# Block 1's first norms: eight leading tiles on x times the norm weight, the token factor put on their PSUM banks

## The reference

```
def rmsnorm(x, g):
    y = x * lax.rsqrt(jnp.mean(x * x, axis=-1, keepdims=True) + EPS)
    return y * g

xn = rmsnorm(x, norm1_g[l])
proj = xn @ w_in                      # 1024 x 9472: gdn_qkv (2048 columns), gates and others
gdn_qkv = silu(causal_dwconv(gdn_qkv, conv_w))     # four taps per channel
q, k = l2norm(...), l2norm(...)                    # then the gated delta rule
```

## Time and profile before

| | us |
|---|---|
| median of 3 runs (lowest, highest) | 2471.23 (2468.78, 2472.56) |
| the profiled execution | 2476.37 |
| its span | 2474.5 |
| PE busy | 2375.8 (96%) |
| DVE, ACT, POOL busy | 1432.0, 1246.8, 301.3 |
| first product of the lead, layer 0 | 16.80 |
| first product of the lead, layer 1 | 671.92 |

### The profile page before, as it was taken

How to read it: one execution, slowest core, us unless ns; L and a number is a source line. 1 busy time by engine, 2 the same in 40 slices (tenths; PEclk the granted TensorE clock), 3 DMA queues, 4 the chain that set the end, 5 groups by cost and what they waited for, 6 DMA issues and landing times.

```text
span 2474.5 us, 48016 instructions
## 1 busy us (share of the span) xinstructions
PE 2375.8 (96%) x21242; PEld 2197.9 (89%) x21242; DVE 1432.0 (58%) x2151; ACT 1246.8 (50%) x1846; POOL 301.3 (12%) x171
## 2 busy tenths in 40 slices
PE   6989999999999899899999999999999999998999
PEld 6979898999899798899999787887789998787999
DVE  6773875665467467756655247643335553676554
ACT  5745654554466475456544367542223453445543
POOL 5213000000141220001000004200000001331000
PEclk9999999999999999999999999999999999999999
DMA  5344354555444444445553336333325542223555
GB/s 195 127 155 169 137 179 151 198 184 190 164 170 149 153 160 147 173 142 204 189 186 122 119 107 219 119 119 137 119 85 188 205 155 88 81 93 137 176 190 181
DMA packets 55824, 380.98 MB, mean 154 GB/s; under 512 B 6081, under 2 KB 9665, under 8 KB 10305
## 3 DMA queue, kind: packets, MB, share of 16 engines
q1 hardware_dynamic: 54864, 374.59, 42.2%
q10 hardware_dynamic: 752, 3.33, 0.4%
HBM read 375.79 MB, written 1.05 MB: 152 GB/s over the span
## 4 chain that ended last, share of the span: by engine, by line
PE 75%; DVE 12%; ACT 7%; DMA 3%; issue 2%; POOL 0%; DVEq 0%; ACTq 0%; POOLq 0%
PE ps L950 20%; PE ps L951 19%; PE ps L952 19%; DVE r L2241 4%; ACT r L1577 2%; DMA ring<-in_win 2%; PE ps L1031 1%; PE ps L1032 1%; PE ps L1033 1%; PE ps L1079 1%; PE ps L909 1%; PE ps L871 1%; PE ps L988 1%; DVE slab L2330 1%; PE ps L989 1%
## 5 line engine op out<-in xcount | busy, mean ns | idle before, releaser
L950 PE MATMUL ps<-r,r 128*128 128x256 f32 (+1 forms) x4448 | 1321.0, 297 | 11.9 <-DVE r L2241 3.1
L951 PE MATMUL ps<-r,r 128*128 128x256 f32 (+1 forms) x4448 | 1306.5, 294 | 0.0
L952 PE MATMUL ps<-r,r 128*128 128x256 f32 (+1 forms) x4448 | 1305.9, 294 | 0.0
L2241 DVE TENSOR_TENSOR r<-ring,r 128x1024 fp32r<-128x1024 f32 x554 | 678.6, 1258 | 508.9 <-ACT r L1577 508.5
L950 PEld LDWEIGHTS ps<-r,r 128*128 128x128 f32 x4448 | 838.2, 188 | 49.5 <-issue 13.3
L952 PEld LDWEIGHTS ps<-r,r 128*128 128x128 f32 x4448 | 837.9, 188 | 24.9
L951 PEld LDWEIGHTS ps<-r,r 128*128 128x128 f32 x4448 | 838.3, 188 | 24.4 <-issue 0.5
L1577 ACT ACTIVATE r<-ring 128x1024 fp32r<-128x1024 f32 (+1 forms) x610 | 610.1, 1041 | 276.2 <-DMA ring<-in_fo 61.7
L3176 POOL TENSOR_TENSOR slab<-slab 128x512 f32<-128x512 f32 (+1 forms) x20 | 28.7, 1433 | 1234.4 <-ACT slab L1693 1214.1
L3128 POOL TENSOR_TENSOR r<-ring,r 128x1024 fp32r<-128x1024 f32 x56 | 132.7, 2393 | 226.1 <-ACT r L1577 216.2
L2330 DVE SCALAR_TENSOR_TENSOR slab<-ps,v,slab 128x255 f32<-128x255 f32 (+1 forms) x168 | 67.8, 475 | 76.0 <-ACT slab L1645 76.0
(11 more groups left out here) (348 smaller groups left out, 2522.5 us busy)
## 6 DMA issues: line engine op xcount, KB each, us to landing
ring<-in_win SPq DMA_DIRECT2D x74, 1024.0 KB, 4.8
ring<-in_ada SPq DMA_DIRECT2D x48, 1024.0 KB, 4.8
ring<-in_fi SPq DMA_DIRECT2D x44, 1024.0 KB, 4.8
ring<-in_fo SPq DMA_DIRECT2D x36, 1024.0 KB, 4.7
ring<-in_wup SPq DMA_DIRECT2D x32, 1024.0 KB, 4.7
ring<-in_wdn SPq DMA_DIRECT2D x32, 1024.0 KB, 4.7
ring<-in_hin SPq DMA_DIRECT2D x20, 1024.0 KB, 4.7
ring<-in_nqkv SPq DMA_DIRECT2D x12, 1024.0 KB, 4.8
```

The lines of the kernel that those rows point to most:

```text
L950: self.mm(o, hi[:, k - k0, cs], xh, k == 0, False)
L951: self.mm(o, hi[:, k - k0, cs], xl, False, False)
L952: i = self.mm(o, lo[:, k - k0, cs], xh, False, k == last)
L2241: self.tt(K.low(p), K.raw(p), K.high(p).bitcast(F32), ALU.subtract).then_inc(*self.up("w_lo_v", p))
```

## The change

In both layers the first eight tiles of `qkv` (`raw=8`) are multiplied with `xg`, the split of x * g, in place of `xn`. The token factor is put on afterwards: for each of these four banks DVE multiplies the bank in place by `rs` before ACT writes the last tap. `xn` is still made, for everything from `wsm` and tile 8 on.

- In layer 0 ACT loads x itself, in three pieces, with a small load of the norm weight ahead; SP's first unit is split in two loads; the low parts of chunks 0 and 1 are made by DVE in place of POOL. The constants, vectors and other inputs are loaded one unit later.
- PE runs 20 products of ones, 128 columns each, at the start (`awake`).
- In layer 1 `xg` is made tile pair by tile pair while `wdn` of layer 0 adds to x, on ACT and DVE.
- The order of turns: `norm1` is in three steps, with the lead, the product with ones, and tiles 2 and 3 between; `normed` stands behind the first bank's taps; tiles 4 to 7 come before `wsm`; `ada0` of layer 1 comes behind `wsm`; the transposes stand behind tiles 8 and 9, and both `angles` turns, tiles 10 and 11 and the chain to `dA` between them and `cum`, which follows tile 11 at once as before.

```diff
+    def source(self, K, tile):
+        if tile < self.more.get("raw", 0):
+            return K.xg, lambda k: ("n_v", ("lo", ("g", self.layer), k))
+        return self.x, self.xk
...
-        win("qkv", 0, 16, "conv", lead=2, dst=self.g_acc, taps="gw", bias=None, free=[])
+        win("qkv", 0, 16, "conv", lead=2, raw=8, dst=self.g_acc, taps="gw", bias=None, free=[])
...
-    if L:
-        yield ("ada0", 1)
-    yield from [("norm1", None), ("qkv", 2), ("small", 1), ("qkv", 1), ("small", 2), *first(("angles", 1)), ("qkv", 1), ("small", 1), *first(("angles", 1)),
-                ("qkv", 1), *first(("angles", 1)),
-                ("qkv", 1), ("small", 1), *first(("conditions", None)), ("qk", 1), ("qkv", 1), ahead("z", 1), ...
+    yield from [("norm1", 1), ("qkv", 1), ("norm1", 1), ("qkv", 1), ("norm1", None), ("qkv", 2), ("small", 1), *([("ada0", 1)] if L else []),
+                ("qkv", 1), ("small", 2), *first(("angles", 1)), *first(("angles", 1)), ("qkv", 1), ("small", 1), *first(("angles", 1)), ("small", 1), *first(("conditions", None)), ("qk", 1), ("qkv", 1), ahead("z", 1), ...
...
+    def awake(self):
+        P = self.open("awake")
+        for _ in range(AWAKE):
+            self.mm(P[:, 0:128], self.K.one, self.K.one, True, True)
...
     def start(self):                                   # ScalarE
-        self.wait_ge(self.K.sem("x"), 16)
-        self.wait_ge(*self.at("misc_g", "eps"))
+        K = self.K
+        self.e.dma_start(K.gain, K.d["v1"][:, 0, 0:8]).then_inc(K.sem("gain"), 16)
+        for n, (a, b) in enumerate(XIN):
+            self.e.dma_start(K.x[:, a:b, :], K.d["x"][:, a:b, :]).then_inc(K.sem(f"x{n}"), 16)
+        self.e.preload_act_table_set(LN_EXP)
...
+    def gained(self, L, a, b):                         # ScalarE
+        for j in range(a, b):
+            self.act(K.xg[0][:, j, :], K.x[:, j, :], ACT.Copy, scale=K.gain_of(L)[:, j:j + 1])...
...
     def norm(self, pid, own):                          # ScalarE
         if own:
+            for n, (a, b) in enumerate(XIN):
+                self.wait_ge(K.sem(f"x{n}"), 16)
+                self.gained(0, a, b)
+                if n < 2:
+                    self.first(n)
             self.power_own(pid, K.x, T)
...
+        yield
+        self.root(pid, K.rs[:, 0, :], T, 1 / 1024)
         yield
         self.highs(pid, K.sq, K.xn, 8)
...
     def conv(self, job):                               # VectorE
+                if g < job.more.get("raw", 0):
+                    self.wait_ge(*self.at("dense_p", job.key, g))
+                    self.wait_ge(*self.at("n_s", "rs", ("n1", job.layer)))
+                    self.tt(P, P, bc(self.K.rs[:, 0:1, :], [128, m, T]), ALU.mult)...
...
     def onto_x(self, job, g, m, P):                    # VectorE
+        if job.more["power"] == ("n1", 1):
+            self.wait_ge(*self.mine("ev_v"))
+            self.gained(1, g, g + m)
...
     def gained(self, L, a, b):                         # VectorE
+        for j in range(a, b):
+            self.stt(K.xg[1][:, j, :], K.x[:, j, :], K.gain_of(L)[:, j:j + 1], K.xg[0][:, j, :].bitcast(F32), ALU.mult, ALU.subtract)...
```

More of the change, by code:

```diff
@@ L21 @@
 HI = 4
+AWAKE = 20
 AHEAD = 2
@@ L259, in rings @@
             h = 2 * (split[self.unit_of[p]] % 2) + c % 2
-            self.hi_of[p], self.hi_before[p], self.by_pool[p] = h, at.get(h), mat == "win" and c < 28
+            self.hi_of[p], self.hi_before[p], self.by_pool[p] = h, at.get(h), mat == "win" and c < 28 and p > 1
             at[h] = p
@@ L300, in power_wide, with gain_of @@
         return 512 if pid == ("n1", 2) else T
+    def gain_of(self, L):
+        return self.V1[1]["n1"] if L else self.gain
     def presummed(self, pid):
@@ L409, in block1_memory @@
         self.mixed, self.gate, self.y, self.sq, self.rs = (A(8, T) for _ in range(5))
-        self.one = self.mixed[:, 0, 0:128]
+        self.one = self.gate[:, 0, 0:128]
+        at = SHIFT + 2 * 8 * T
+        self.xg = [blocks(self.rounded(at + i, 8 * T), 8) for i in (0, 2 * 8 * T)]
         self.few = self.gate[:, 1:2, :]
@@ L971, in lead @@
         halves, got = job.more.get("halves"), {}
+        source, have = job.source(K, 0)
         if halves:
@@ L975, in lead @@
             whole, by_tile = slice(0, n), job.more.get("by_tile", kt)
-            order = [(whole, job.xk, t, k) for k in range(by_tile) for t in range(tiles)]
-            order += [(whole, job.xk, t, k) for t in range(tiles) for k in range(by_tile, kt)]
+            order = [(whole, have, t, k) for k in range(by_tile) for t in range(tiles)]
+            order += [(whole, have, t, k) for t in range(tiles) for k in range(by_tile, kt)]
         for cs, xk, t, k in order:
@@ L1755, in norm @@
         if own:
-            self.power_own(pid, K.x, T)
-            self.e.preload_act_table_set(LN_EXP)
-            self.first(0)
-            self.log(pid, K.rs[:, 0, :], T, 1 / 1024)
-            self.roots(pid, K.rs[:, 0, :])
-            self.first(1)
-        else:
-            self.root(pid, K.rs[:, 0, :], T, 1 / 1024)
+            self.wait_ge(K.sem("gain"), 16)
+            for n, (a, b) in enumerate(XIN):
[3 more added lines that the diff above has]
+                    self.first(n)
+            self.power_own(pid, K.x, T)
+        yield
+        if own:
+            self.wait_ge(*self.at("misc_g", "eps"))
+        self.root(pid, K.rs[:, 0, :], T, 1 / 1024)
         yield
@@ L1814, in angles @@
             self.wait_ge(*self.at("misc_v", name))
-            self.act(tab, K.y[:, 2, :] if name == "cos" else K.y[:, 4, :], ACT.Sin).then_inc(*self.up("misc_s", name))
+            self.act(tab, K.around[:, 2, :] if name == "cos" else K.around[:, 4, :], ACT.Sin).then_inc(*self.up("misc_s", name))
             yield
@@ L2430, in norm @@
             self.tt(both[:, 0, :], both[:, 0, :], both[:, 1, :], ALU.add).then_inc(*self.up("n_v", "sum", pid))
-            for p in range(2):
-                self.first(p)
+        yield
         yield
@@ L2455, in angles @@
         self.ts(ang, pos, K.V1[0]["inv"], None, ALU.mult).then_inc(*up("misc_v"))
-        for name, shift, kk, r in (("cos", 0.25, K.y[:, 1, :], K.y[:, 2, :]), ("sin", 0.0, K.y[:, 5, :], K.y[:, 4, :])):
+        for name, shift, kk, r in (("cos", 0.25, K.around[:, 1, :], K.around[:, 2, :]), ("sin", 0.0, K.around[:, 5, :], K.around[:, 4, :])):
             self.wait_ge(*mine("misc_v"))
@@ L3276, in program @@
             at = 2 * (u % RAW) * SLOT
+            if u == 0:
+                e.dma_start(K.ring[:, 0:SLOT], src[:, 0:SLOT]).then_inc(K.sem("head"), 16)
+                e.dma_start(K.ring[:, SLOT:2 * SLOT], src[:, SLOT:2 * SLOT]).then_inc(K.raw_sem(chunks[1]), 16)
+                continue
             e.dma_start(K.ring[:, at:at + src.shape[1]], src).then_inc(K.raw_sem(chunks[0]), 16)
```

47 lines of the change are left out of this document (31 added, 16 removed).

## The result

| | before | forecast | after |
|---|---|---|---|
| median, us | 2471.89 (4 runs) | 2482 (2466 to 2491) | 2498.30 (4 runs, 2496.74 to 2501.76) |
| profiled execution / its span | 2476.37 / 2474.5 | 2487.3 | 2501.76 / 2499.9 |
| pieces of x at ACT, layer 0 | 6.33 (whole) | 4.3, 5.3, 7.4 | 9.80, 12.76, 17.00 |
| product with ones | 10.48 | 16.2 | 24.64 |
| tile 6, layer 0 | | 32.7 | 41.35 |

The ratio after to before is 1.0112, 95% interval 1.0099 to 1.0124. The direction was right, the size was not: the time lies 7 us above the top of the range. The spans differ by 25.4 us: +15.6 up to tile 14 of layer 0, -1.4 from there to the end of `wdn` (590.0 in place of 591.4), +11.7 from there to tile 14 of layer 1, -0.5 behind it.

The account below looks back on a forecast made before the run. PE, busy 96% of the span, was taken as the bound, so only its pauses and low clock count. Layer 0 +3.2 and layer 1 +7.7 gave +10.9 us on 2471.2: 2482, range 2466 to 2491.

Parts of the forecast that it names:

- Start of layer 0: Layer 0's start: x arrives in pieces by 7.4, the lead ends at 15.6 in place of 24.2, a gain of 8.6 us.
- the fifth rival: Start: x not earlier because it shares with the weights, first products 2 us later, 2484; chance 0.56 together with the forecast.
- I take no spell: Between products of ones and lead, layer 0: no low-clock stretch after pauses of 0.9 and 1.7 us; 1.5 to 2.8 otherwise.
- A new wait at tile 6: Tile 6, layer 0 and again layer 1: PE waits 4.7 us (4 to 5.5) for chunk 6, prepared behind `xn`.
- A longer wait at `cum`: `cum` of layer 0: PE waits 10 us (5.5 to 11.7) where it waited 2.27, one bank covering in place of three.
- Step into layer 1: From `wdn` into layer 1: PE goes straight into the lead, 665.0 to 670.6 at full clock; tile 7 ends at 694.5.
- A wait for the ring: Tile 8 of layer 1: the load of chunks 8 and 9 is issued late, PE waits 4.3 us (3.5 to 4.7).
- `cum` of layer 1: At `cum` in layer 1, without angles: PE waits 3.8 us (2 to 5) for the chain to `dA`.
- a spell 1.5: Behind a new pause: products run at 1.2 GHz for a while, priced at 1.5 us from a span of 1.5 to 2.8.
- my fourth rival: Slower still: each of five pauses is followed by 29 products at 1.2 GHz, +6.5 us over the forecast, 2489; chance 0.17.
- Nothing is given back: Behind tile 14: old order, DVE's and ACT's chains as late as PE, so none of the added time is recovered.

Follow-up runs that it names:

- The remedies: Two runs, each against the changed kernel: x loaded from SP's queue, 2491.55 us; SP's second unit held back until x is there, 2494.40 us.
- the fastest kernel: Changed kernel plus x on SP, chunks 6 and 7 ahead, `ada0` behind, `cum` later, and chunks of `wsm`, 8, 9 right behind `xn`: 2469.38 us, ratio 0.9985.

## Why the prediction was right in direction and too small

By the spans 25.4 us were measured and 10.9 forecast: 14.5 are missing.

**Step "Start of layer 0": wrong, 8.4 of the 14.5 us.** I took the pieces of x at 4.3, 5.3 and 7.4, "with -1 to +2 us on all", because all of x landed by 6.33 when it went ahead of everything. It no longer does: the new order asks for x and 4.2 MB of SP's at once. The pieces came 5.5, 7.5 and 9.6 us later than that, and the product with ones at 24.64 in place of 16.2; from it to tile 6 the forecast holds (16.7 against 16.5). That the lateness is sharing is shown by the run in which the second unit waits. The Trainium skill, "DMA: Bandwidth & Descriptors", section on queues, rings and completion order, has each DMA engine taking its issuers' rows in turn, a packet at a time. The traces agree: in the run with x in one load, whose first 25 us hold no other loads, SP's 4.18 MB are 864 packets of the profile and ACT's 1.05 MB 1184; taken in turn x, a fifth of the bytes, must be the last to land, and it was (16.8 there, 17.0 in the changed kernel). I had cited it and put it at 2 us, and the fifth rival named this case at the same price: the mistake was not to divide the bytes asked for by the rate in the earlier trace rows, 295 GB/s, which gives 18 us for 5.2 MB (the first us without a byte included). The remedies give back 4 of the 8.4 us; the rest of the step's miss stays open.

**"I take no spell" behind the products of ones: wrong.** The pauses were 4.9 and 1.9 us and the clock was at 1.2 GHz behind both. The forecast's 1.5 us for a warm start were not there, as the run with one product shows.

**"A new wait at tile 6": right.** 4.81 and 4.83 against 4.7 (4 to 5.5), released by POOL's low part, and the edit that moves chunks 6 and 7 ahead removes it. The forecast priced only the first wait: `wsm` is late behind it, a second pause in the shadow of the first.

**"A longer wait at `cum`": right in place, at the far end in size.** 11.6 against 10 (5.5 to 11.7). I had allowed POOL two or three holds of 2.3 and taken 65; three came, two in the second chain of angles and one on `dA` itself. From the transposes to `cum` 18.8 us passed, 2.0 more than forecast.

**Step into layer 1: right.** PE goes straight from `wdn` into the lead, and no time is lost or won against the forecast up to tile 6 (22.9 against 22.4).

**"A wait for the ring": right.** 4.69 against 4.3 at tile 8, and moving `ada0` takes it away. `cum` of layer 1: 4.5 against 3.8.

**Term "a spell 1.5" (low clock): too small, about 4 of the 14.5 us.** From tile 6 to the transposes 16.7 us passed in layer 0 where five tiles at full clock take 14.0; I had added 1.5. The five stretches behind the pauses, without the pauses, took 1.2, 0.4, 0.2, 0.8 and 1.1 us more than forecast. The forecast took the short end of the earlier trace rows; my fourth rival (the text also calls it the third) took the long end for all, and its 6.5 us were a little nearer to these 3.7. The Trainium skill, "TensorE: Matmul & The Clock Gate", Part 1, says that the number of products at the lower clock varies between runs; the runs agree: 25 products lie 0.21 us apart behind the pause at tile 6 of layer 0, 16 behind that of layer 1 and 21 behind tile 8's. A forecast of five pauses must take the middle, not the end.

**"Nothing is given back" behind tile 14: not contradicted.** The two stretches came out 1.4 and 0.5 us shorter. But such stretches differ by 8 us and more between profiles of kernels with the same order there, so that they are this near is partly luck.

Sum: forecast +10.9; start +8.4, tile 6 and clock +1.4, up to `cum` of layer 0 +2.0 and behind it +0.4, layer 1 +4.0, the rest -1.9: 25.2 of the 25.4 measured. The range had given the start only 2 us above, and one step shifted everything behind it. The forecast had +3.2 for layer 0 and +7.7 for layer 1 and measured were +15.6 and +11.7: right in sign and in where PE waits, wrong in the size of the start above all.

## What to carry to other kernels

When a load is moved to another queue, add up all the bytes asked for at the same time, by every queue, and divide by the rate the trace shows; a load's old landing time belongs to its old place in the order. Count the cover at both ends of what is moved: the new order starts the lead early and leaves one bank of cover in place of three at `cum`, and single turns of the list (two chunks prepared earlier, `ada0` later) won 7.8 and 4.8 us by the marks. A removed pause is judged by what is late next, so measure from mark to mark in the profile, not by totals alone, and set the last mark behind the stage that the edit can still delay: `cum` a bank later won 7.5 us at the `qk` sums and 1.4 six tiles on.

## What the runs showed of the hardware beyond what was expected

- Two queues shared the DMA engines such that 1 MB of x, issued by 2.8 us, landed with the last of 5.2 MB, at 17.0; without the second unit it landed by 9.96.
- A DVE instruction with a single SBUF input is held behind POOL as well: L2553, 16 columns, 0.17 us alone, took 2.35.
- A short pause may or may not be followed by low clock. In the fastest kernel the granted clock is 0.70 in the 4 us from 13.0, behind a pause of 2.4 at 11.56, and 0.71 in the 2.9 us from 38.1, behind the 2.23; but it is 1.00 in the 3 us behind the longer pauses of 2.57 at 58.05 and 2.62 at 726.68. In these rows the length of the pause alone doesn't decide it.
